# Norms without a normalised copy: raw rows transposed by products with a diagonal, in a two-layer encoder kernel

## The reference

```python
def rms_norm(x, g):
    y = x * lax.rsqrt(jnp.mean(x * x, axis=-1, keepdims=True) + EPS)
    return y * g

h = h + mixer(rms_norm(h, ln_mix[l]))
h = h + cross_attention(rms_norm(h, ln_cross[l]), rms_norm(mem, ln_mem[l]), ...)
h = h + hier_moe(rms_norm(h, ln_ffn[l]), ...)      # top-1 group, top-2 experts inside it
out = rms_norm(h, ln_final)                        # after the last layer
```

## Time and profile before

| What | us |
|---|---|
| Median of three runs | 1202.43 |
| Profiled execution, whole | 1199.93 |
| Its span | 1198.1 |
| PE busy in the span | 1075.8 (90%), 4468 matmul records |
| PEld busy | 642.3 (54%) |
| DVE busy | 289.8 (24%) |
| ACT busy | 177.7 (15%) |

### The profile page before, as it was taken

The page is one execution under the profiler, slowest core; times in us unless marked ns, Lnnn a source line. Parts: engine busy times, 40 slices in busy tenths (PEclk is TensorE's granted clock), DMA queues, the critical chain, the costliest instruction groups (busy, mean ns, idle before and its releaser), DMA issues.

```text
span 1198.1 us, 10951 instructions
## 1 busy us (share of the span) xinstructions
PE 1075.8 (90%) x4468; PEld 642.3 (54%) x4468; DVE 289.8 (24%) x716; ACT 177.7 (15%) x367; POOL 11.1 (1%) x21
## 2 busy tenths in 40 slices
PE   3999698989999999699999999997877799999985
PEld 3567357464444443278767777685363544444432
DVE  5124332440111111402121222022324301111114
ACT  3014311111111110111110111011021111111100
POOL 1020000000000000000000000000000000000000
PEclk9999899989999999899999999998999799999998
DMA  9763134118999999994391761952051099999991
GB/s 326 258 198 148 64 121 160 71 71 347 427 427 429 427 427 427 232 248 87 80 252 23 185 169 15 302 205 76 0 211 37 35 381 422 429 428 428 427 424 60
DMA packets 107095, 284.09 MB, mean 237 GB/s; under 512 B 4631, under 2 KB 82535, under 8 KB 94505
## 3 DMA queue, kind: packets, MB, share of 16 engines
q1 hardware_dynamic: 104656, 279.72, 63.0%
q0 software_dynamic: 1168, 3.40, 1.1%
q10 hardware_dynamic: 1224, 0.30, 0.1%
HBM read 282.30 MB, written 1.11 MB: 237 GB/s over the span
## 4 chain that ended last, share of the span: by engine, by line
issue 93%; PE 3%; DMA 2%; DVE 1%; POOL 1%; DVEq 0%; ACT 0%; SPq 0%; POOLq 0%
PE banks L910 3%; DMA scratch<-mem_in 1%; DMA scratch<-ln_final_in 0%; DMA bias_rows<-scratch 0%; PE banks L913 0%; DVE scratch L1615 0%; POOL rw L880 0%; POOL rw L882 0%; DVE nrm L1494 0%; DVE nrm L1482 0%; DVE nrm L1491 0%; DVEq L103 0%; POOL rb L884 0%; DVE tmp L1456 0%; POOL rb L885 0%
## 5 line engine op out<-in xcount | busy, mean ns | idle before, releaser
L910 PE MATMUL banks<-ring,scratch 128*64 128x512 f32 (+1 forms) x1760 | 437.7, 598 | 13.1 <-DMA ring<-expert_w_up_in 5.4
L910 PEld LDWEIGHTS banks<-ring,scratch 128*64 128x64 f32 (+1 forms) x1760 | 163.1, 145 | 277.3 <-issue 274.3
L910 PE MATMUL banks<-nT,ring 128*128 128x256 f32 x1104 | 242.9, 382 | 4.7 <-ACT nT L592 1.9
L910 PEld LDWEIGHTS banks<-nT,ring 128*128 128x128 f32 x1104 | 211.2, 192 | 34.8 <-DVE nT L594 2.7
L910 PE MATMUL banks<-ring,nT 128*128 128x384 f32 (+2 forms) x352 | 118.1, 491 | 1.0 <-ACT nT L592 1.0
L910 PEld LDWEIGHTS banks<-ring,nT 128*128 128x128 f32 x352 | 64.7, 193 | 46.7 <-issue 15.2
L913 PE MATMUL banks<-cst,nrm 128*128 128x128 f32 x176 | 32.9, 339 | 51.0 <-DVE nrm L1526 24.1
L666 ACT ACTIVATE scratch<-banks 128x512 f32<-128x512 f32 (+1 forms) x84 | 47.5, 585 | 203.8 <-PE banks L910 112.0
L910 PE MATMUL banks<-scratch 128*128 128x256 f32 (+3 forms) x280 | 62.1, 409 | 14.1 <-ACT scratch L666 11.8
L1764 DVE TENSOR_TENSOR h<-banks,h 128x512 f32<-128x512 f32 x64 | 44.3, 692 | 121.7 <-PE banks L1226 119.2
L910 PE MATMUL banks<-scratch,nrm 128*128 128x256 f32 x256 | 61.7, 398 | 2.3 <-DVE scratch L1716 2.3
(11 more groups left out here) (154 smaller groups left out, 430.1 us busy)
## 6 DMA issues: line engine op xcount, KB each, us to landing
ring<-expert_w_gate_in SPq DMA_DIRECT2D x32, 2048.0 KB, 13.1
ring<-expert_w_up_in SPq DMA_DIRECT2D x32, 2048.0 KB, 14.4
ring<-expert_w_down_in SPq DMA_DIRECT2D x32, 2048.0 KB, 12.2
ring<-odd_w_in_in SPq DMA_DIRECT2D x72, 512.0 KB, 7.0
ring<-xkv_w_in SPq DMA_DIRECT2D x4, 2048.0 KB, 12.7
ring<-even_w_in_in SPq DMA_DIRECT2D x3, 2048.0 KB, 20.8
scratch<-bias_rows SPq DMA_DIRECT2D x8, 576.0 KB, 7.9
ring<-even_w_out_in SPq DMA_DIRECT2D x2, 2048.0 KB, 10.1
```

Source lines behind the costliest of these rows:

```text
L910: return giving_back(nc.tensor.matmul(dst, lhsT, rhs, start=start, stop=stop))
```

## The change

The norms m and 1 to 6 no longer write scaled rows for the transposition. DVE writes, for each tile, a 128x128 diagonal matrix `diag[:, t]` with the inverse roots on its diagonal (identity times a per-partition scalar). PE makes each block of `nT` by one product: the stationary operand is the raw chunk of `h` (or of the memory's rows), read in place with a step of eight elements, the moving operand is the diagonal. Norms 3 and 6, which the gathers read, still write normalised rows, both tiles now by ACT, contiguous in channels, tile 0 ahead of its evacuations and tile 1 behind them; the gathers wait for a new semaphore `nrm_set` and read `nrm` with a step of eight as stationary operand. Norm 7 is as before. Three semaphores (`nrm0`, `nrm1a`, `nrm1`) give way to two (`diag_set`, `nrm_set`).

```diff
-        nrm = sb("nrm", [P, TILES, CH, P])
+        nrm = sb("nrm", [P, TILES, D])
+        diag = sb("diag", [P, TILES, P])
...
         def rows(t):
-            return nrm[:, t].rearrange("p c q -> p (c q)")
+            return nrm[:, t]
+
+        def chunk(rows_of, t, c):
+            return rows_of[:, t].rearrange("p (q c) -> p c q", c=CH)[:, c, :]
...
# ACT, norm(name)
-                act.wait_ge(rstd_set, i + 1)
-                nc.scalar.activation(nrm[:, 1, :, 64:P].rearrange("p c q -> p q c"),
-                                     src[:, 1, 512:D].rearrange("p (q c) -> p q c", c=CH),
-                                     ACT.Copy, scale=rst[:, 1:2]).then_inc(nrm1, 1)
+                if name in "36":
+                    act.wait_ge(rstd_set, i + 1)
+                    nc.scalar.activation(rows(0), src[:, 0, :], ACT.Copy, scale=rst[:, 0:1])
                 middle()
                 evacuate_norm(act, True, name)
+                if name in "36":
+                    nc.scalar.activation(rows(1), src[:, 1, :], ACT.Copy, scale=rst[:, 1:2]).then_inc(nrm_set, 1)
...
# PE, norm(name)
-                pe.wait_ge(nrm0, i + 1)
-                pe.wait_ge(nrm1a, i + 1)
-                pe.wait_ge(nrm1, i + 1)
+                pe.wait_ge(diag_set, 2 * i + 2)
...
-                            last = flip(pbank(k)[:, at:at + P], nrm[:, t, c, :])
+                            last = mm(pbank(k)[:, at:at + P], chunk(NORMS[name][0], t, c), diag[:, t, :], True, True)
...
# PE, gather(g, j)
+                    pe.wait_ge(nrm_set, l + 1)
                     pe.wait_ge(sel_set, GROUPS * l + g + 1)
...
-                            last = mm(pbank(k)[:, i * 256:(i + 1) * 256], nrm[:, t, 2 * j + i, :],
+                            last = mm(pbank(k)[:, i * 256:(i + 1) * 256], chunk(nrm, t, 2 * j + i),
...
# DVE, norm(name)
-                if i:
-                    dve.wait_ge(nrm1, i)
+                def on_diagonal(t):
+                    v.tensor_scalar(diag[:, t, :], ident, rst[:, t:t + 1], None, ALU.mult).then_inc(diag_set, 1)
...
-                        v.tensor_scalar(nrm[:, 0].rearrange("p c q -> p q c"),
-                                        src[:, 0, :].rearrange("p (q c) -> p q c", c=CH),
-                                        rst[:, 0:1], None, ALU.mult).then_inc(nrm0, 1)
...
                     variance(0)
                     step(rsqrt([0]))
-                    scale0()
+                    on_diagonal(0)
...
-                v.tensor_scalar(nrm[:, 1, :, 0:64].rearrange("p c q -> p q c"),
-                                src[:, 1, 0:512].rearrange("p (q c) -> p q c", c=CH),
-                                rst[:, 1:2], None, ALU.mult).then_inc(nrm1a, 1)
+                on_diagonal(1)
                 middle()
                 evacuate_norm(dve, False, name)
```

More of the change, by code:

```diff
@@ L160, in encoder @@
         q4 = a.take(4 * SEQ).rearrange("p (b s) -> p b s", b=4)
-        prob = nrm.rearrange("p t c q -> p (t c q)").rearrange("p (n t k) -> p n t k", n=4, t=2)
+        prob = nrm.rearrange("p t d -> p (t d)").rearrange("p (n t k) -> p n t k", n=4, t=2)
         probT = a.take(4 * 2 * 256).rearrange("p (n b q) -> p n b q", n=4, b=2)
@@ L255, in encoder @@
         rstd_set = sem("rstd_ready")
-        nrm0 = sem("tile0_normalised")
-        nrm1a = sem("tile1_first_half_normalised")
-        nrm1 = sem("tile1_second_half_normalised")
+        diag_set = sem("scale_on_diagonal_ready")
+        nrm_set = sem("normalised_rows_ready")
         piece_ready = sem("piece_in_psum")
@@ L531, in _ @@
                 sp.wait_ge(fin_set, t + 1)
-                sp.dma_start(out[0, t * P:(t + 1) * P, :], nrm[:, t].rearrange("p c q -> p (c q)")).then_inc(out_done, 16)
+                sp.dma_start(out[0, t * P:(t + 1) * P, :], nrm[:, t]).then_inc(out_done, 16)
             sp.wait_ge(out_done, 16 * TILES)
@@ L1310, in second_pass @@
                                 for t in range(TILES):
-                                    last = mm(bank[2 + c // 4][:, (c % 4) * P:(c % 4 + 1) * P], nrm[:, t, c, :],
+                                    last = mm(bank[2 + c // 4][:, (c % 4) * P:(c % 4 + 1) * P], chunk(nrm, t, c),
                                               selr[:, t, :], t == 0, t == 1)
@@ L1488, in scale0 @@
                 def scale0():
[L1489 to L1493, removed]
-                        v.tensor_scalar(nrm[:, 0].rearrange("p c q -> p q c"),
-                                        src[:, 0, :].rearrange("p (q c) -> p q c", c=CH),
-                                        rst[:, 0:1], None, ALU.mult).then_inc(nrm0, 1)
+                    dve.wait_ge(lnf_in, 16)
+                    v.scalar_tensor_tensor(out=rows(0), in0=src[:, 0, :], scalar=rst[:, 0:1], in1=lnf,
+                                           op0=ALU.mult, op1=ALU.mult).then_inc(fin_set, 1)
                 if at is None:
@@ L1505, in norm @@
                     dve.wait_ge(rstd_set, i + 1)
-                    scale0()
+                    if name == "7":
+                        scale0()
+                    else:
+                        if name == "m":
+                            dve.wait_ge(id_in, 16)
+                        on_diagonal(0)
                 else:
@@ L1586, in layer_norm_values @@
                     step(v.bn_aggr(aggr[:, t, :], stats[:, t, :]))
-                dve.wait_ge(nrm1, NORM_SEQ["1"] + 1)
                 step(v.tensor_scalar(var[:, :], aggr[:, :, 1], EPS, None, ALU.add))
```

## The result

The changed kernel takes 1223.07 us (median of 4 runs, 1220.48 to 1231.03) against 1202.45 us for the kernel before beside it: ratio 1.0191, interval 1.016 to 1.0221. The profiled execution took 1220.48 us with a span of 1218.7, against 1199.93. The forecast of 1204.3 is wrong, and the time lies above the range of 1197.5 to 1217 too: the change costs 20.6 us where +1.9 was expected.

The account below looks back on a forecast made before the run. PE was taken as the bound, a little ahead of the weight stream, with a DVE-PE-evacuation chain in the norms. 9.65 us added, 4.5 taken, 3.3 from the clock: about +1.9, 1204.3 us; range with 8 in 10, 1197.5 to 1217.

Parts of the forecast that it names:

- The step of eight: Strided loads of stationary operands in norms and gathers: taken at no cost, between bounds of none and twice the load's time.
- its whole sum: All terms over the whole kernel: +5.15 us before the clock, less 3.3 from the clock, +1.85 us.
- ACT's row: Nearest price for a step: ACT writing 512 elements strided, 1259 ns, against 1024 without, 1059; over twice per element.
- Rival 1: The strided load costs double in the norms: 12.8 us more, +14.7 with the sum, 1217 us in all; chance 0.24.
- Door 1: The DMA port swizzle: Cited rule for SBUF reads: 16-byte lines, a penalty per new line, four float32 free, so a step of eight is beyond.
- The gathers: Their strided loads hide under a 0.219 us record and cost nothing; if double just fails to hide, up to 5 us.
- the sign of being wrong: The prediction called itself wrong if, among other signs, the gathers came slower than 0.22 us a record.
- The earlier start: PE starts sooner without the wait for scaling: 1.3 us each in norms m and 4, 0.95 in 5 and 6; 4.5 taken.
- The expert stages: Their length was to stay unchanged; a change there would show the prediction wrong.
- The second record of each block: In the norms a block's product takes two records, a transposition one: 9.65 us added before the clock.
- The clock: Behind norms 3 and 1 a higher PE clock was to give back half of the loss, 3.3 us.
- The clock behind norm 3: TensorE at 1.2 GHz for 10.2 us loses 5.1 us of PE; half, 2.5, was taken as regained.

Follow-up runs that it names:

- Experiment 1: The changed kernel with each chunk read as 128 neighbouring elements, without the step, in norms and gathers: 1201.89 us against 1202.23 for the kernel before, ratio 0.9999.
- experiment 9: The kernel before with normalised rows left in row order, so scaling writes contiguously and transpositions and gathers read with a 32-byte step: 1205.37 us, ratio 1.002.
- experiments 4 to 6: The changed kernel with only the norms read without the step (ratio 1.0032), with only the gathers read so (1.0158), and unaltered on the same chip (1.0166).
- experiment 8: The kernel before with its transpositions made as ordinary products with the identity, nothing strided: 1206.76 us against 1202.56, ratio 1.0034.

## Why the prediction was wrong, by its steps

**The step that failed** is the one under "The step of eight": "I take no cost, since a record of 128 columns gets one element each 0.112/128 = 0.9 ns, slow for a read." With the step an element takes 0.24/128 = 1.9 ns, at either clock, and the load, not the moving side, sets the pace. Experiment 1 takes away the step alone and with it the whole 20 us. So the term that the prediction put at nothing was worth about ten times its whole sum. What misled was the choice between ACT's row (over twice per element with a step) and VectorE's (the same): the second compared a strided 1024-element write with a 256-element operation whose source and place differ. The like comparison is experiment 9, 753 ns against 1.41 us. Compared like with like, both engines spoke for nearly a doubling (ScalarE 0.722 us against 1.26), though of writes; no row before priced a read by TensorE.

**Rival 1** named the mechanism, with a chance of 0.24, and was too small: 0.21 us a record against 0.24, and above all "about 1 in each of the four others, where the clock is low and a record takes 0.21 anyway". The four cold norms cost 1.95 + 2.5 + 2.8 + 3.1 = 10.3 us net, where 4 x 1.8 - 4.5 + 4 = 6.7 was its sum. Against experiment 1, which has the same start and no step, the step adds 1.3, 1.2, 1.9 and 2.5 us there from first block to next product. Since the strided load is blind to the clock, the part of the norm that ran at 2.4 GHz was lost as well. Norms 2 and 3 lost 4.4 each, where it had 0.8 + 3.2 = 4.0.

The Trainium skill, page "SBUF — State Buffer", section "Door 1: The DMA port swizzle", was cited for a penalty beyond four float32. The direction agrees with the runs; the bound doesn't. Four float32 are already over the cliff (329 ns against 196 for two). The same passage also asks for at least two accesses to each line of 16 bytes, and that form agrees with the runs: a step of 8 bytes has two to a line, one of 16 has one. Seen from the result, 0.24 was too little for its rule.

**The gathers** "cost nothing by either bound" failed in its own terms: 0.245 us a record against 0.219, the sign of being wrong that the prediction named. The bracket behind it, "up to 5 us", holds the 0 to 4.1 us of experiments 4 to 6.

**What was right.** The earlier start: PE begins 883.27 - 882.88 = 0.39 us behind the last Newton step in norm 5 (0.45 forecast), 0.54 in norm 4 (0.6), and 1.38 us earlier in norm m (1.3). With the step away it is worth some 4.5 us by experiments 8 and 1, as in the sum. The expert stages kept their length, as forecast: 238.7 us against 238.5 in layer 0, and in layer 1, from the first expert product to PE's last, 232.7 against 231.4, within what the other traces spread (230.9 to 233.5).

**What was right by offsets.** Together, experiment 1 (ratio 0.9999) answers to the forecast's "+1.9" within what can be told, but two terms of it were off and cancelled, which is luck. The second record of each block had 9.65 before the clock and measured 10.7 in the traces of experiment 8. The clock was to give back 3.3 (2.5 behind norm 3, 0.8 behind norm 1) and gave 4.9 there: 1.6, 1.2, and 2.0 behind norm m, which the prediction didn't look at. What is left of the two, 5.8 us in one pair of traces, stands against 4.2 between the medians; executions of the kernel before alone differ by more than that gap (1199.92 to 1206.83).

**The clock behind norm 3** rose from a mean of 0.63 (238 to 252) to 0.79 (252 to 268, both above): low for about 10.2 us before, 2 x 0.21 x 16 = 6.7 now. That gives PE 1.7 us of the 5.1 back, a third where the half was taken (2.5). Behind norm 1 the first 32 products took 79.56 - 65.75 = 13.8 us against 76.01 - 60.76 = 15.2 before, 1.4 gained, and 1.6 was lost again by 115 us; 0.8 was taken.

## What to carry to other kernels

Before a TensorE operand is read with a step, look for its load in the trace beside the record that must hide it: with a step of 16 or 32 bytes a 128-element float32 operand of a product needs about 0.24 us here, which only a record longer than that hides (a transposition's load, 190 ns, was no trouble). Let neighbours stay within 8 bytes where the layout is free. Compare a strided row only with the same operation on the same number of elements. And where a norm's chain is shortened, compare the granted clock of all executions, not of one trace each, before the gain is booked.

## What the runs showed of the hardware

- The stationary float32 operand of a 128x128 product loads in 192 ns without a step, 196 with a step of 8 bytes, 329 with 16 and 335 with 32 (at 2.4 GHz); with 32 bytes it is 338 ns at 1.2 GHz too. A moving operand with a step of 32 bytes holds a record of 128 columns to 0.233 us; steps of 8 and 16 bytes were not tried there.
- A transposition's load is 140 ns, 190 with the step of 32 bytes.
- Contiguous float32 loads follow the clock, 192 ns at 2.4 GHz and 333 at 1.2.
- At 1.2 GHz the step costs little: the loads of norm 4 start every (523.0 - 518.9)/17 = 0.24 us with it and every (508.8 - 504.8)/19 = 0.21 without. At 2.4 GHz it doubles the record, 0.24 against 0.112.
- Writes with a step of 512 bytes cost VectorE 1.41 us for 1024 elements against 0.75 contiguous, ScalarE 1.26 against 0.72 for 512.
